# Tile by tile ahead of five norms: the last unit of a projection split in two, with VectorE squaring its own sums

## The chip, the cores and the metric

The kernel runs on one core of one Trainium2 chip. The metric is the device time of one execution in microseconds, given as the median of several runs. Every stage of the network runs in one launch, with the engines tied together by semaphores written by hand.

## What is computed

A stack of small transformer-like layers on a sequence of T = 256 tokens with D = 1024 channels, all in 32-bit floats. Between the stages the residual stream `x` goes through RMS norms:

```python
def _rmsnorm(x, g):
    xf = x.astype(jnp.float32)
    y = xf * lax.rsqrt(jnp.mean(xf * xf, axis=-1, keepdims=True) + EPS)
    return (y * g.astype(jnp.float32)).astype(x.dtype)
```

The parts around the change, with their norms as the kernel numbers them:

```python
x = x + gate_m * ((z @ w_glu_a) * sigmoid(z @ w_glu_b))              # glu, then norm 3
x = x + gate_f * (square(relu(h @ w_fc1)) @ w_fc2)                   # fc2_1, then norms 4 and 5 (norm_f, then the next block's)
h = h + mamba2_mixer(h, ...)                                         # ... @ out_w is ssm_out, then norm 6
h = h + sigmoid(rms_norm(h, ple_norm_w) @ gate_w) * (p @ proj_w)     # ple_gate_0, then norm 7
h = h + attention(h, ...)                                            # ... @ attn_out_w is attn_out, then norm 8
```

## The kernel before, in words

**Layout.** The residual stream `xT` is kept with channels on the 128 partitions: eight tiles `xT[:, k]` of 128x256. A projection's output is computed in units of two tiles (128 x 2 x 256, 512 values a partition, one PSUM bank). Weights arrive in blocks of 1024 x 256 in a ring of four. A matrix product in full precision is made of three products in a rounded format: ScalarE rounds a block (`round_to`, L869), VectorE takes the rest of it (`lower_to`, L2319, two instructions of 128x1024 a block), the same is done to the input, and TensorE runs high x high, high x low, low x high (`block_products`, L1473, L1494 to L1498). fc1_1 and fc2_1 do the first two as one product 512 wide (`wide_products`, L1506, L1520 and L1521), with each of a unit's two tiles in a bank of its own.

**Order inside a unit.** `project` (L1533) finishes the first tile before it starts the second. In ssm_out (L2165) and fc2_1 (L2051) the two tiles alternate at every k. The consumer of a unit waits for `blocks_done`, which rises when the last block of the unit is through, so it always sees both tiles at once.

**A norm.** When VectorE has added a unit to two tiles of `xT` (L2830 and L2834 in glu, L2390 in fc2_1, L3072 in `add_projection`, L3087 and L3089 in `embedding`), it raises `x_ready`. ScalarE then squares these two tiles (`square`, L918, one instruction of 128x512 at L926) and raises `sq_ready`. TensorE multiplies the squares by a matrix of ones (`norm_stats`, L1680, L1691), which sums over channels and leaves the sum on all partitions: eight tiles, each of two passes for an ordinary 32-bit product. For norms 0, 1, 2, 4, 6, 7 and 8 VectorE first adds the squares of the first units (`sum_squares`, L2397, with L2403 and L2406), so that TensorE has four tiles instead of eight; norm 3 has all eight. At norm 4 TensorE multiplies all eight tiles by other weights for the first of two norms (L1707) and uses the added squares for the second (L1711 to L1714). ScalarE takes Ln and Exp of the result (L943 or L941, L944) to make `rstd`, VectorE normalises the eight tiles (L2839, L2903, L2889, L2882), ScalarE rounds each (L889, L891), and TensorE's next block begins with the first rounded tile (`swept`, `swept_wide`).

**What stands in the queues around it.** The order on each engine is written out by hand. TensorE: at norms 6 and 8 it has products of the embedding (`ple_unit`, L2182) between the last block and the statistics. At norms 3, 4, 7 and 8 it has products that nobody reads (`idle_products`, L1675, L1678): four ahead of norm 7's statistics, five behind those of norms 3 and 7, two behind norm 4's, one behind norm 8's. ScalarE: at norm 3 it rounds the first block of fc1_1 and loads the table for Ln and Exp (L914) ahead of the four squares. At norm 7 it takes the Sigmoid of a unit (L1359) first, then loads the table, then squares. VectorE: the lowering of the next stage's first block stands ahead of the last unit in fc2_1 (`residual_halves`, L2378), and behind it at ssm_out and attn_out.

A few lines of the glu stage on VectorE, and of norm 3 on ScalarE:

```python
ps = unit("glu", 2 * n + 1)                                   # waits for the whole block
tt(glu_prod, ps, glu_gate, ALU.mult).then_inc(glu_mul, 1)     # L2830, 128x512
for i in range(2):                                            # L2834, two of 128x256
    ins = nc.vector.scalar_tensor_tensor(out=xT[:, k], in0=glu_prod[:, i], scalar=mod(1, GATE_M, k), in1=xT[:, k], ...)
ins.then_inc(x_ready, 1)

def norm_squares(i, version):
    log_and_exp()                                             # L914, a table load
    for p in range(4):
        square(i, version, p)                                 # L926, waits for x_ready
```

Of the kernel before, what the change touches and what calls it, by code (L numbers as in the profile page):

```python
# [10 lines left out]

# [221 lines left out]
def program(nc, dram, out):  # L233
# [8 lines left out]
    with ctx:  # L242
# [55 lines left out]
        STAT, MISC = PS[4], PS[5:8]  # L298
        SPARE = PS[3]
# [90 lines left out]
        hn_ready = sem("hn_ready")  # L390
        h_ready = sem("h_ready")
# [50 lines left out]
        rows_act = sem("rows_act")  # L442
        rows_dve = sem("rows_dve")
# [242 lines left out]

        def wide_units(phase, blocks_each, leaves):
# [25 lines left out]
        for layer, version in ((0, 7), (1, 9)):  # L713
# [14 lines left out]
            units(f"ple_gate_{layer}", 1, [(ple_sig, 4 * layer + n + 1) for n in range(4)])  # L728
# [129 lines left out]
        def _(act):  # L858
# [291 lines left out]
            ins.then_inc(rows_act, 1)  # L1150
# [83 lines left out]
            square(4, 4, 3)  # L1234
# [96 lines left out]
            def embedding(phase, layer, norm, version):  # L1331
                for p in range(4):
                    round_to(ready[first_unit[phase] + p] + 1 if p < 3 else first_block[f"ple_gate_{layer}"] + 1)
                    square(norm, version, p)
# [17 lines left out]
                for n in range(4):  # L1352
# [13 lines left out]
            square(7, 7, 3)  # L1366
# [92 lines left out]
        def _(pe):  # L1459
# [13 lines left out]
            def block_products(phase, n, arrived, places):  # L1473
# [29 lines left out]
                if places[-1][2].stop == NB:  # L1503
                    last.then_inc(blocks_done, 1)

            def wide_products(phase, n, arrived, places):  # L1506
# [4 lines left out]
                for k, ps, columns, x_high, x_low, start, stop in places:  # L1511
# [4 lines left out]
                    if arrived and columns.start == 0:  # L1516
# [5 lines left out]
                                            start=False, stop=stop, skip_group_check=True)  # L1522
                last.then_inc(blocks_done, 1)
# [9 lines left out]
            def project(phase, n, x, arrived=None, unit=None, order=range(KB)):  # L1533
# [4 lines left out]
                                for i in range(2) for k in order])  # L1538

# [140 lines left out]
            def norm_stats(i):  # L1680
# [17 lines left out]
            def two_norm_stats():  # L1698
# [5 lines left out]
                for k in range(DT):  # L1704
                    if k % 2 == 0:
# [242 lines left out]
            pe.wait_ge(rows_act, 1)  # L1948
            pe.wait_ge(rows_dve, 1)
# [99 lines left out]
            for n in range(4):  # L2049
                ps = wide_banks("fc2_1", n)  # L2050
                for kb in range(4):  # L2051
                    tile = split_arrived("fc2_1", 2) if n == 0 else None
                    wide_products("fc2_1", 4 * n + kb, (lambda k: tile(KB * kb + k)) if tile else None,
                                  [(k, ps[i], slice(P * i, P * i + P), hid_high[:, KB * kb + k], hid[:, KB * kb + k],
                                    kb == 0 and k == 0, kb == 3 and k == KB - 1)
                                   for k in range(KB) for i in range(2)])
# [103 lines left out]
            for kb in range(2):  # L2160
                for n in range(4):
                    if kb == 0:
                        banks.append(pair(start_unit("ssm_out", n)))
                    arrived = split_arrived("ssm_out") if n == 0 else None
                    block_products("ssm_out", 4 * kb + n, (lambda k: arrived(KB * kb + k)) if arrived else None,  # L2165
                                   [(k, banks[n][:, i], slice(P * i, P * i + P), at_tile((y_high, xs), KB * kb + k),
                                     kb == 0 and k == 0 and i == 0, kb == 1 and k == KB - 1)
                                    for k in range(KB) for i in range(2)])
# [17 lines left out]
            def embedding(layer, norm):  # L2186
# [1096 lines left out]
```

## Time and profile before

| | |
|---|---|
| median of 3 runs | 1170.21 us (1169.49 to 1174.09) |
| the profiled execution, its own time | 1172.47 us |
| its span, first to last instruction | 1170.6 us |
| mean granted TensorE clock | 0.982 |
| TensorE busy (matmul) | 1113.4 us, 95% of the span |
| VectorE busy | 829.1 us, 71% |
| ScalarE busy | 558.1 us, 48% |
| GpSimd busy | 45.0 us, 4% |
| DMA, mean | 210 GB/s |

The time of an execution is 1.87 us longer than the span of its profile. Matmuls are pipelined: an instruction's duration overlaps the next one's, so the distance between starts is what counts. A matmul of 32-bit operands shows as two passes (x2). In the chain of waits, each line has a start, the time that this piece adds to the chain, and what it was.

### The profile page before, as it was taken

To read this page: it belongs to the slowest core of one execution; us is meant where nothing else is said; L and a number is where in the kernel's file an instruction comes from. 1 tells how busy PE (TensorE), PEld (TensorE's weight loads), DVE (VectorE), ACT (ScalarE), POOL (GpSimd) and SP (SyncE) were. 2 spreads that over 40 slices of the span, in tenths; PEclk is the share of its full clock that TensorE was granted. 3 is DMA by queue.
4 is the path that set the end of the run, shared out by engine and by line. 5 is a ranking of instruction groups with operands and counts; after the bars stand their busy time and mean duration, and the time that the engine had idled before them with its cause. 6 is when DMAs were issued, how large, how long until landed. Compare 5 with 4: busy or idle time off the path is not lost.

```text
span 1170.6 us, 21137 instructions
## 1 busy us (share of the span) xinstructions
PE 1113.4 (95%) x8970; PEld 971.9 (83%) x8970; DVE 829.1 (71%) x1414; ACT 558.1 (48%) x876; POOL 45.0 (4%) x71
## 2 busy tenths in 40 slices
PE   7899898999999997879999999999989999999998
PEld 4788676988888885469988888899978899988898
DVE  1699466877578674875677764578898966659955
ACT  3224633445101124653555543456677846467944
POOL 0010011000000000000000000000000000042000
PEclk9999998999999998999999999989999999999999
DMA  9977688899848957865455555525432345343342
GB/s 374 377 279 270 229 327 305 306 333 329 342 181 251 346 191 157 329 246 180 144 180 184 187 194 190 180 80 173 158 130 78 133 151 180 130 152 117 107 145 72
DMA packets 38287, 246.41 MB, mean 210 GB/s; under 512 B 4400, under 2 KB 5584, under 8 KB 9648
## 3 DMA queue, kind: packets, MB, share of 16 engines
q1 hardware_dynamic: 29072, 182.36, 45.8%
q0 software_dynamic: 6240, 43.94, 9.9%
q10 hardware_dynamic: 2880, 18.74, 3.9%
q8 instruction: 71, 1.16, 0.4%
q14 instruction: 24, 0.20, 0.1%
HBM read 225.24 MB, written 19.79 MB: 209 GB/s over the span
## 4 chain that ended last, share of the span: by engine, by line
PE 78%; DVE 10%; DMA 5%; ACT 4%; issue 2%; SPq 0%; ACTq 0%; DVEq 0%
PE ps L1494 11%; PE ps L1498 10%; PE ps L1496 10%; PE ps L1520 10%; PE ps L1501 10%; PE ps L1521 5%; PE ps L1645 4%; DMA ca_dram<-more 2%; PE ps L1738 1%; DMA more<-in_ada_w 1%; PE ps L2182 1%; PE ps L1593 1%; DVE ada_more L2974 1%; PE ps L1691 1%; PE ps L1871 1%
## 5 line engine op out<-in xcount | busy, mean ns | idle before, releaser
L1494 PE MATMUL ps<-rounded_parts,w_high_rounded 128*128 128x256 f32 x1136 | 328.9, 290 | 2.2 <-DVE rounded_parts L2335 1.3
L2328 DVE TENSOR_TENSOR ring_rounded<-ring,w_high_rounded 128x1024 fp32r<-128x1024 f32 x220 | 260.8, 1227 | 88.9 <-ACT w_high_rounded L882 88.5
L1496 PE MATMUL ps<-rounded_parts,w_high_rounded 128*128 128x256 f32 x1136 | 322.9, 284 | 0.0
L1498 PE MATMUL ps<-rounded_parts,ring_rounded 128*128 128x256 f32 x1136 | 322.8, 284 | 0.0
L882 ACT ACTIVATE w_high_rounded<-ring 128x1024 fp32r<-128x1024 f32 x220 | 219.8, 1049 | 63.8 <-PE ps L1521 48.2
L1494 PEld LDWEIGHTS ps<-rounded_parts,w_high_rounded 128*128 128x128 f32 x1136 | 219.6, 193 | 11.4 <-issue 6.7
L1496 PEld LDWEIGHTS ps<-rounded_parts,w_high_rounded 128*128 128x128 f32 x1136 | 219.6, 193 | 0.2
L1498 PEld LDWEIGHTS ps<-rounded_parts,ring_rounded 128*128 128x128 f32 x1136 | 219.4, 193 | 0.0
L1520 PE MATMUL ps<-rounded_parts,w_high_rounded 128*128 128x512 f32 x496 | 175.3, 399 | 0.0
L1521 PE MATMUL ps<-rounded_parts,ring_rounded 128*128 128x256 f32 x496 | 139.3, 281 | 0.0
L1501 PE MATMUL ps<-big,ring 128*128 128x256 f32 x544 | 121.0, 381 | 0.0
L1501 PEld LDWEIGHTS ps<-big,ring 128*128 128x128 f32 x544 | 102.1, 190 | 14.7 <-issue 1.2
L1520 PEld LDWEIGHTS ps<-rounded_parts,w_high_rounded 128*128 128x128 f32 x496 | 93.2, 188 | 23.3
L1521 PEld LDWEIGHTS ps<-rounded_parts,ring_rounded 128*128 128x128 f32 x496 | 93.7, 189 | 0.0
L2460 DVE SCALAR_TENSOR_TENSOR big<-big,cols 128x256 f32<-128x256 f32 x120 | 48.0, 479 | 0.0
L1079 ACT ACTIVATE we_t<-ps 128x512 f32<-128x512 f32 x32 | 17.4, 596 | 58.0 <-PE ps L1871 58.0
L1501 PE MATMUL ps<-hT,ring 128*128 128x256 f32 x192 | 42.7, 381 | 0.0
L1501 PEld LDWEIGHTS ps<-hT,ring 128*128 128x128 f32 x192 | 36.1, 190 | 6.4 <-issue 1.2
L1060 ACT ACTIVATE big<-ps 128x512 f32<-128x512 f32 x16 | 9.6, 598 | 64.8 <-PE ps L1498 55.4
L2928 DVE SCALAR_TENSOR_TENSOR ada_w<-ada_w,cols 128x256 f32<-128x256 f32 x72 | 29.6, 482 | 8.4 <-ACT ada_w L1254 8.4
L1645 PE MATMUL ps<-ada_w,ada_more 128*32 128x256 f32 x432 | 29.3, 389 | 4.1 <-DMA ada_w<-in_ada_w 4.1
L926 ACT ACTIVATE sq<-xT 128x512 f32<-128x512 f32 x24 | 14.3, 623 | 36.4 <-DVE xT L3072 27.4
(426 smaller groups left out, 1555.1 us busy)
## 6 DMA issues: line engine op xcount, KB each, us to landing
ring<-in_blocks SPq DMA_DIRECT2D x139, 1024.0 KB, 4.9
ada_w<-in_ada_w POOLq DMA_DIRECT2D x27, 1024.0 KB, 7.5
ada_more<-in_ada_w POOLq DMA_DIRECT2D x13, 1024.0 KB, 7.5
we_dram<-we_t ACTq DMA_DIRECT2D x8, 1024.0 KB, 7.8
ca_dram<-more ACTq DMA_DIRECT2D x8, 1024.0 KB, 10.8
ring<-we_dram SPq DMA_DIRECT2D x8, 1024.0 KB, 5.7
ring<-ca_dram SPq DMA_DIRECT2D x8, 1024.0 KB, 7.2
big<-in_ada_w SPq DMA_DIRECT2D x4, 1024.0 KB, 11.3
```

The lines of the kernel that those rows point to most:

```text
L882: nc.scalar.activation(w_high[:, c % 2, ks], ring[:, b % RING, ks], ACT.Copy)\
L1079: nc.scalar.activation(we_t[:, 2 * b:2 * b + 2].rearrange("p g r x -> p (g r x)"), MISC[b % 2][:, :], ACT.Copy).then_inc(we_copied, 1)
L1494: nc.tensor.matmul(out, high[:, k, columns], x_high, start=start, stop=False, skip_group_check=True)
L1496: nc.tensor.matmul(out, high[:, k, columns], x_low, start=False, stop=False, skip_group_check=True)
L1498: last = nc.tensor.matmul(out, low[:, k, columns], x_high, start=False, stop=stop, skip_group_check=True)
L1501: last = nc.tensor.matmul(out, w[:, k, columns], x, start=start, stop=stop, skip_group_check=True)
L1520: nc.tensor.matmul(ps[:, :], w_hi[:, k, columns], both, start=start, stop=False, skip_group_check=True)
L1521: last = nc.tensor.matmul(ps[:, T * first:T * first + T], w_lo[:, k, columns], rounded(x_high), start=False, stop=stop, skip_group_check=True)
L1645: last = nc.tensor.matmul(bank[j:j + COPIES, 0:NB], c_spread[:, k, PIECES - 1 - piece:PIECES - 1 - piece + COPIES], w[:, k], start=(piece ...
L2328: nc.vector.tensor_tensor(rounded(w), w, w_high[:, c % 2, ks], ALU.subtract)\
L2460: ins = nc.vector.scalar_tensor_tensor(out=conv[:, k], in0=apad[:, k, tap:tap + T], scalar=w, in1=conv[:, k], op0=ALU.mult, op1=ALU.add)
L2928: ins = nc.vector.scalar_tensor_tensor(out=dst, in0=src[:, i, tap:tap + T], scalar=w, in1=dst, op0=ALU.mult, op1=ALU.add)
```

## The change

The last unit ahead of norms 3, 4, 6, 7 and 8 is computed and consumed tile by tile.

TensorE finishes the first tile of the unit's last block before the second, and raises a new semaphore, `tile_done`. Except in fc2_1, where it has been so, the second tile goes into another bank (`LAST_TILE`, the first half of bank 7). VectorE waits for the first tile alone, adds it to `xT` and squares it itself (`square_tile`), and does the same with the second when the block is done. ScalarE's square of the last two tiles goes. At ple_gate_0 ScalarE's Sigmoid of the last unit is two of 128x256. TensorE's statistics wait for each of the two last squares. Norm 3 joins the norms whose first six squares are added up by VectorE; that sum stands ahead of the tile work. In fc2_1 the lowering of the first xbc block moves behind the last unit. Two semaphores of the S5 stage become one.

```diff
+        LAST_TILE = MISC[2][:, 0:T]
...
-        sq_before = (0, 4, 8, 12, 16, None, 20, 24, 28)
-        summed = {0: 3, 1: 3, 2: 2, 4: 3, 6: 3, 7: 3, 8: 3}
-        sums_until = {i: n + 1 for n, i in enumerate(summed)}
+        sq_before = (0, 4, 8, 12, 15, None, 18, 21, 24)
+        summed = {0: 3, 1: 3, 2: 2, 3: 3, 4: 3, 6: 3, 7: 3, 8: 3}
+        TAILS = (3, 4, 6, 7, 8)
+        tail_of = {i: n + 1 for n, i in enumerate(TAILS)}
+        sums_until = {i: n + 1 + 2 * sum(t < i for t in TAILS) for n, i in enumerate(summed)}
...
             def norm_squares(i, version):
                 log_and_exp()
-                for p in range(4):
+                for p in range(3 if i in TAILS else 4):
                     square(i, version, p)
...
             log_and_exp()
-            square(4, 4, 3)
             norm_rstd(4)
...
-                    square(norm, version, p)
+                    if p < 3:
+                        square(norm, version, p)
...
-                    ps = unit(f"ple_gate_{layer}", n)
                     if n >= 2:
                         act.wait_ge(ple_mul, 4 * layer + n - 1)
+                    if layer == 0 and n == 3:
+                        act.wait_ge(tile_done, tail_of[7])
+                        nc.scalar.activation(ple_gate[:, 1, 0:T], bank_of(first_unit["ple_gate_0"] + 3)[:, 0:T],
+                                             ACT.Sigmoid).then_inc(ple_sig, 1)
+                        unit("ple_gate_0", 3)
+                        nc.scalar.activation(ple_gate[:, 1, T:2 * T], LAST_TILE, ACT.Sigmoid).then_inc(ple_sig, 1)
+                        continue
+                    ps = unit(f"ple_gate_{layer}", n)
...
             log_and_exp()
-            square(7, 7, 3)
             norm_rstd(7)
...
+                    if tail and stop and columns.start == 0:
+                        last.then_inc(tile_done, 1)
                 last.then_inc(blocks_done, 1)
...
+            def project_tail(phase, n, x):
+
+                outs = start_unit(phase, n)[:, 0:T], LAST_TILE
+                tile_products(phase, n, [[(k, outs[i], slice(P * i, P * i + P), at_tile(x, k), k == 0, k == KB - 1)
+                                          for k in range(KB)] for i in range(2)])
+
+            def tile_products(phase, n, halves):
+
+                block_products(phase, n, None, halves[0]).then_inc(tile_done, 1)
+                block_products(phase, n, None, halves[1])
...
                     if k == 0 and i in summed:
                         pe.wait_ge(sq_sum, sums_until[i])
+                    elif i in TAILS and k >= 6:
+                        pe.wait_ge(sq_sum, sums_until[i] + k - 5)
                     elif k % 2 == 0:
...
-            for n in range(8):
+            for n in range(7):
                 project("glu", n, (sq, mixT), split_arrived("glu", 2) if n == 0 else None)
+            project_tail("glu", 7, (sq, mixT))
             norm_stats(3)
...
-                                   for k in range(KB) for i in range(2)])
+                                   for k, i in sorted(itertools.product(range(KB), range(2)),
+                                                      key=lambda at: at[1] if tail else 0)], tail)
...
+                    outs = [banks[n][:, 0], LAST_TILE if n == 3 else banks[n][:, 1]]
...
+                    if kb == 1 and n == 3:
+                        tile_products("ssm_out", 4 * kb + n, halves)
...
+                    elif layer == 0 and n == 3:
+                        project_tail("ple_gate_0", 3, (sq, hT))
...
+            project_tail("attn_out", 3, (att_high, mixT))
...
+            def square_tile(i, k):
+
+                nc.vector.tensor_tensor(squares(i)[:, k], xT[:, k], xT[:, k], ALU.mult).then_inc(sq_sum, 1)
+
+            def tail_tile(i, phase, n, first):
+
+                if first:
+                    dve.wait_ge(tile_done, tail_of[i])
+                    return bank_of(first_unit[phase] + n)[:, 0:T]
+                dve.wait_ge(blocks_done, ready[first_unit[phase] + n])
+                return LAST_TILE
...
                 dve.wait_ge(glu_sig, n + 1)
+                if n == 3:
+                    sum_squares(3)
+                    dve.wait_ge(x_ready, 8 + 3)
+                    for i in range(2):
+                        ins = tt(glu_prod[:, i], tail_tile(3, "glu", 7, i == 0), glu_gate[:, i], ALU.mult)
+                        if i:
+                            ins.then_inc(glu_mul, 1)
+                            dve.wait_ge(glu_mul, 4)
+                        else:
+                            link(ins)
+                        ins = nc.vector.scalar_tensor_tensor(out=xT[:, 6 + i], in0=glu_prod[:, i],
+                                                             scalar=mod(1, GATE_M, 6 + i), in1=xT[:, 6 + i],
+                                                             op0=ALU.mult, op1=ALU.add)
+                        if i:
+                            ins.then_inc(x_ready, 1)
+                            dve.wait_ge(x_ready, 8 + 4)
+                        else:
+                            link(ins)
+                        square_tile(3, 6 + i)
+                    continue
...
             sum_squares(4, final_sum)
-            residual_halves("fc2_1", gate_f1, 3, 4)
+            lower_to(ready[first_unit["fc2_1"] + 6])
+            for i in range(2):
+                if i == 0:
+                    dve.wait_ge(tile_done, tail_of[4])
+                else:
+                    dve.wait_ge(blocks_done, ready[first_unit["fc2_1"] + 6])
+                for half in range(2):
+                    ins = nc.vector.scalar_tensor_tensor(out=xT[:, 6 + i], in0=bank_pair("fc2_1", 3)[:, i, half],
+                                                         scalar=gate_f1(6 + i), in1=xT[:, 6 + i], op0=ALU.mult, op1=ALU.add)
...
+                square_tile(4, 6 + i)
...
-                for n in range(4):
+                for n in range(3):
                     nc.vector.tensor_tensor(xT[:, 2 * n:2 * n + 2], xT[:, 2 * n:2 * n + 2], unit(phase, n), ALU.add)\
                         .then_inc(x_ready, 1)
-                    if n == 2:
-                        sum_squares(norm)
+                sum_squares(norm)
+                for i in range(2):
+                    ins = nc.vector.tensor_tensor(xT[:, 6 + i], xT[:, 6 + i], tail_tile(norm, phase, 3, i == 0), ALU.add)
...
+                    square_tile(norm, 6 + i)
```

In `embedding` on VectorE the last unit of layer 0 becomes the same per tile: product with the gate (128x256), sum into `xT`, `square_tile(7, 6 + i)`, each waiting for the one before. `wait_ge(rows_act, 1)` and `wait_ge(rows_dve, 1)` become `wait_ge(rows_copied, 2)`.

## Rows read from the trace of the kernel before

**Rows 1.** The page: busy time and instructions; the chain's shares by engine.

```profile
PE 1113.4 (95%) x8970; PEld 971.9 (83%) x8970; DVE 829.1 (71%) x1414; ACT 558.1 (48%) x876; POOL 45.0 (4%) x71
...
PE 78%; DVE 10%; DMA 5%; ACT 4%; issue 2%; SPq 0%; ACTq 0%; DVEq 0%
```

**Rows 2.** The chain in order of time at norms 3, 4, 6, 7, 8: start, us, what.

```profile
567.53 3.49 PE ps L1691 x16
...
755.48 3.55 PE ps L1707 x16
...
976.63 3.46 PE ps L2182 x16
980.09 1.73 PE ps L1691 x8
...
1012.23 2.16 PE ps L1678 x10
...
1136.46 1.73 PE ps L1691 x8
```

**Rows 3.** Timeline of ScalarE at norm 3: start us, us, instruction [idle before <-releaser].

```profile
564.32 1.28 ACT L914 ACT_TABLE_LOAD   x1
565.61 1.68 ACT L926 ACTIVATE big<-xT 128x512 f32<-128x512 f32 x3
569.21 0.63 ACT L926 ACTIVATE big<-xT 128x512 f32<-128x512 f32 x1 [1.93 <-DVE xT L2834]
```

**Rows 4.** Timeline of VectorE ahead of norms 3, 4 and 6.

```profile
563.45 2.36 DVE L2328 TENSOR_TENSOR ring_rounded<-ring,w_high_rounded 128x1024 fp32r<-128x1024 f32 x2 [3.52 <-ACT w_high_rounded L882]
...
751.02 2.36 DVE L2328 TENSOR_TENSOR ring_rounded<-ring,w_high_rounded 128x1024 fp32r<-128x1024 f32 x2 [3.29 <-ACT w_high_rounded L882]
...
972.29 0.69 DVE L2403 TENSOR_TENSOR sq<-sq 128x512 f32<-128x512 f32 x1 [0.70 <-ACT sq L926]
973.02 0.69 DVE L2406 TENSOR_TENSOR sq<-sq 128x512 f32<-128x512 f32 x1
```

**Rows 5.** Groups by line and form on VectorE: xcount | busy us, mean ns | idle.

```profile
L2961 DVE TENSOR_TENSOR more<-ps,we_t 128x256 f32<-128x256 f32 x16 | 5.9, 420 | 0.4 <-PE ps L2067 0.4
...
L2834 DVE SCALAR_TENSOR_TENSOR xT<-more,mods,xT 128x256 f32<-128x256 f32 x8 | 3.5, 482 | 0.1
```

**Rows 6.** Timeline of TensorE and ScalarE at norm 7.

```profile
1008.14 1.89 PE L1678 MATMUL ps<-const 128*128 128x256 f32 x8
1009.87 1.03 PE L1691 MATMUL ps<-big,const 128*128 128x256 f32 x4
1011.10 1.13 PE L1691 MATMUL ps<-big,const 128*128 128x256 f32 x4 [0.21 <-ACT big L926]
...
1010.42 0.63 ACT L926 ACTIVATE big<-xT 128x512 f32<-128x512 f32 x1 [0.18 <-DVE xT L3089]
```

**Rows 7.** Timeline of ScalarE at norms 4, 6 and 8: the last squares.

```profile
757.21 0.63 ACT L926 ACTIVATE sq<-xT 128x512 f32<-128x512 f32 x1 [3.67 <-DVE xT L2390]
...
977.39 0.63 ACT L926 ACTIVATE sq<-xT 128x512 f32<-128x512 f32 x1 [3.23 <-DVE xT L3072]
...
1135.49 0.63 ACT L926 ACTIVATE sq<-xT 128x512 f32<-128x512 f32 x1 [3.23 <-DVE xT L3072]
```

**Rows 8.** Stretches: us, PE, PEld, DVE, ACT, POOL busy (x), granted clock, DMA share, GB/s.

```profile
560.00:567.50 7.50, 7.50 (x64) 7.50 (x64) 2.36 (x2) 5.45 (x7) 0.00 (x0) 1.00 0.42 146
...
874.00:876.00 2.00, 0.74 (x4) 0.54 (x6) 2.00 (x4) 2.00 (x3) 0.00 (x0) 0.80 0.70 274
876.00:878.00 2.00, 2.00 (x12) 1.10 (x10) 2.00 (x3) 1.97 (x3) 0.00 (x0) 0.50 0.53 221
...
882.00:884.00 2.00, 2.00 (x18) 2.00 (x18) 2.00 (x4) 2.00 (x3) 0.00 (x0) 0.99 0.00 0
```

**Rows 9.** Timeline of TensorE: first products after two gaps elsewhere.

```profile
505.97 0.77 PE L2002 MATMUL ps<-const,big 128*128 128x128 f32 x5 [1.88 <-ACT big L1182]
...
875.26 1.13 PE L2090 MATMUL ps<-ada_more,more 128*64 128x256 f32 x4 [2.30 <-DVE ada_more L3021]
```

More of the change, by code:

```diff
@@ L12 @@
+import itertools
 from contextlib import ExitStack
@@ L390, in program @@
         hn_ready = sem("hn_ready")
+        tile_done = sem("tile_done")
         h_ready = sem("h_ready")
@@ L685, in units, with gates_until @@
                 left.append(leave)
+        def gates_until(layer, n):
+            return 5 * layer + n + 1 + (layer == 0 and n == 3)
         def wide_units(phase, blocks_each, leaves):
@@ L727, in program @@
                 ready[first_unit[f"ple_proj_{layer}"] + i] = first_block[f"ple_proj_{layer}"] + 1
-            units(f"ple_gate_{layer}", 1, [(ple_sig, 4 * layer + n + 1) for n in range(4)])
+            units(f"ple_gate_{layer}", 1, [(ple_sig, gates_until(layer, n)) for n in range(4)])
         units("final", 0, [(out_copied, n + 1) for n in range(4)])
@@ L1504, in block_products, with wide_products @@
                     last.then_inc(blocks_done, 1)
-            def wide_products(phase, n, arrived, places):
+                return last
+            def wide_products(phase, n, arrived, places, tail=False):
                 b = first_block[phase] + n
@@ L2052, in _ @@
                     tile = split_arrived("fc2_1", 2) if n == 0 else None
+                    tail = n == 3 and kb == 3
                     wide_products("fc2_1", 4 * n + kb, (lambda k: tile(KB * kb + k)) if tile else None,
@@ L2164, in _ @@
                     arrived = split_arrived("ssm_out") if n == 0 else None
[L2165 to L2168, printed above, removed]
+                    outs = [banks[n][:, 0], LAST_TILE if n == 3 else banks[n][:, 1]]
+                    halves = [[(k, outs[i], slice(P * i, P * i + P), at_tile((y_high, xs), KB * kb + k),
+                                kb == 0 and k == 0 and (i == 0 or n == 3), kb == 1 and k == KB - 1) for k in range(KB)]
+                              for i in range(2)]
+                    if kb == 1 and n == 3:
+                        tile_products("ssm_out", 4 * kb + n, halves)
+                    else:
+                        block_products("ssm_out", 4 * kb + n, (lambda k: arrived(KB * kb + k)) if arrived else None,
+                                       [place for both in zip(*halves) for place in both])
                     if kb == 0 and n < 2:
@@ L3070, in add_projection @@
                 dve.wait_ge(x_ready, 4 * (norm - 1))
-                for n in range(4):
+                for n in range(3):
                     nc.vector.tensor_tensor(xT[:, 2 * n:2 * n + 2], xT[:, 2 * n:2 * n + 2], unit(phase, n), ALU.add)\
                         .then_inc(x_ready, 1)
-                    if n == 2:
-                        sum_squares(norm)
+                sum_squares(norm)
+                for i in range(2):
+                    ins = nc.vector.tensor_tensor(xT[:, 6 + i], xT[:, 6 + i], tail_tile(norm, phase, 3, i == 0), ALU.add)
+                    if i:
+                        ins.then_inc(x_ready, 1)
+                        dve.wait_ge(x_ready, 4 * norm)
+                    else:
+                        link(ins)
+                    square_tile(norm, 6 + i)
             add_projection("ssm_out", 6)
@@ L3083, in embedding @@
                     lower_to(first_block[f"ple_gate_{layer}"] + min(n + 2, 4))
-                    dve.wait_ge(ple_sig, 4 * layer + n + 1)
+                    if layer == 0 and n == 3:
+                        for i in range(2):
+                            dve.wait_ge(ple_sig, 4 + i)
+                            a = ple_prod[:, 6 + i]
+                            ins = nc.vector.tensor_tensor(a, a, ple_gate[:, 1, T * i:T * i + T], ALU.mult)
+                            if i:
+                                ins.then_inc(ple_mul, 1)
+                                dve.wait_ge(ple_mul, 4)
+                            else:
+                                link(ins)
+                            ins = nc.vector.tensor_tensor(xT[:, 6 + i], xT[:, 6 + i], a, ALU.add)
+                            if i:
+                                ins.then_inc(x_ready, 1)
+                                dve.wait_ge(x_ready, 28)
+                            else:
+                                link(ins)
+                            square_tile(7, 6 + i)
+                        continue
+                    dve.wait_ge(ple_sig, gates_until(layer, n))
                     g = ple_gate[:, n % 2].rearrange("p (k n) -> p k n", k=2)
```

20 lines of the change are left out of this document (13 added, 7 removed).

## The prediction, made before the change was run

> **What bounds the kernel now.** I read the page first, then the chain of waits in order of time, then the timelines of each engine around the five norms, and last the granted clock. On the page TensorE is busy 95% of the span and holds 78% of the chain that ended last, VectorE only 10% and ScalarE 4% [rows 1]. So an edit on VectorE or ScalarE is worth only what it takes out of TensorE's waits, and these stand in the stretches between a projection's last block and the next one. In the chain these stretches are TensorE's too [rows 2]. At norms 6 and 8 TensorE works off products of the embedding (3.46 us at norm 6) and then four tiles of statistics, 1.73 us for 8 passes, so one tile costs 0.43 us. At norm 3 it works off all eight tiles (16 passes) in 3.49 us, at norm 4 in 3.55 us; eight tiles without a wait are 2 x 1.73 = 3.46 us. Only norm 7 shows a wait: its first two tiles end at 1010.90, the last two start at 1011.10 and take to 1012.23 [rows 6].
>
> **Norm 7** (the embedding's gate unit 3). Now: block ends about 1008.30, then four idle products and two tiles (1008.14 to 1010.90), and ScalarE's squares end at 1010.42 + 0.63 = 1011.05 [rows 6]; the last two tiles end 1.18 us later. After: the first tile's Sigmoid, product, sum and square lie under the block's second half. For the second tile ScalarE's half-width Sigmoid is some 0.4 us (estimate: 0.42 us is what VectorE needs for this width [rows 5]; ScalarE needs 0.63 for a whole one [rows 6]), then VectorE has a product, a sum and a square of 128x256, each 0.42 us with 0.04 us to the next dependent one [rows 4, 5]: squares stand at 1008.30 + 0.4 + 3 x 0.46 = 1010.1. TensorE starts its tiles only at 1008.30 + 1.73 (four idle products at 0.43) = 1010.03 and reaches the last one 1.3 us after that, so nothing is waited for: end 1010.03 + 1.73 = 1011.76 against 1012.23. **Gain 0.47 us.** What ends last next is the five idle products behind (2.16 us [rows 2]) and the K/V projection after them; both move with it.
>
> **Norm 4** (fc2_1). Now TensorE's eight tiles take 3.55 instead of 3.46 us: ScalarE's squares end at 757.21 + 0.63 = 757.84, just when TensorE wants them [rows 2, 7]. After, they are ready earlier, but TensorE still has its eight tiles: **gain 0.09 us**, and no more. The change also moves the lowering of xbc block 0, 2.36 us, from 751.02 [rows 4], where VectorE was idle, to behind the tail. The tail's second tile is two dependent scalings (0.52 each) and a square (0.46) from 755.5: 757.0; dt_w's lowering 0.4, then 2.36: about 759.8. The normalising waits for rstd, which comes some 1.0 us after the statistics' end at 755.48 + 3.55 = 759.03, thus 760.0. It is hidden with 0.2 us to spare; without cover it costs what it overruns. The swapped order of products inside block 15 costs nothing: same count, and its operands were lowered before the block began.
>
> **Norms 6 and 8.** Squares end at 977.39 + 0.63 = 978.02 and at 1135.49 + 0.63 = 1136.12 [rows 7]. TensorE takes up the first tile of statistics at 980.09 and 1136.46 and the fourth 1.3 us later [rows 2]. They were hidden by 1.7 us and more; making them 0.5 us earlier is worth **0**. The same holds for the second tile's own bank and for the joined semaphore (two waits for one).
>
> **Norm 3** (glu unit 7) is where the sum is decided. The change adds norm 3 to those whose first six tiles VectorE adds up to two, and it puts this sum ahead of the tile work in VectorE's queue. The sum needs ScalarE's three squares; these stand behind a table load at 564.32 (1.28 us) and run 565.61 to 567.29 [rows 3]. The block itself ends at 567.53, its first tile, 24 of its 48 products earlier (64 in 7.5 us, 0.12 us each [rows 8]), at 567.53 - 2.8 = 564.7. So VectorE, free from 565.81 [rows 4], sits behind that wait until 567.3: the first tile is not done meanwhile. Then, strictly in order: two linked sums of 128x512, each 0.69, 0.73 apart [rows 4]: to 568.75. First tile, from 568.67 (its product is independent of the sum, and such an instruction starts 0.08 before the end of the one ahead: in scaling's row four pairs of 2 x 0.48 cover 3.5 us, 0.88 a pair [rows 5]): product 0.46, scaling 0.48 + 0.04 = 0.52, square 0.34: 1.32, to 570.0. Second tile: product 0.46, scaling 0.52, square 0.42: 1.40, to 571.4. From the squares to the end of the statistics norm 7's row gives 1.18 us for two tiles, 0.43 less for one: 0.75. End 572.15. Before it was 567.53 + 3.49 = 571.02. **Loss 1.1 us.** TensorE has 4 x 0.43 = 1.7 us less to do here, but all of that becomes idle time. Behind it every step (Ln, Exp, eight normalisings, roundings, the swept block) moves by the same; the five idle products move too. Bounds: 0.8 us if the three independent instruction starts each overlap by 0.08, 1.5 us if each of the eight steps costs 0.05 more.
>
> The Trainium skill (Perfetto Trace Analysis, Optimizing Scalar/DVE Operations) puts VectorE's per-instruction overhead at some 60 ns from SBUF and 125 ns from PSUM, and advises larger operations. By the rows halving costs more: 2 x 0.42 against 0.69 us [rows 4, 5] is 0.15 us per split operation. With the page's figures the three splits of norm 3 would cost 0.25 us, not 0.46, and the loss there would be 0.9 us; the measured rows decide.
>
> **Sum.** 1.1 - 0.47 - 0.09 = +0.5 us. The profiled execution took 1172.47 us, of which the span is 1170.6; the sum would make it 1173.0. It lies 2.3 us above the median of three, 1170.21, so on the scale of the runs the forecast is **1170.7 us**. The three runs lie 4.6 us apart; a measurement of this kernel can tell some 0.5% (5.9 us) from no change, so this is "no change".
>
> **Rivals.**
> *Every hand-off counts* (faster). The hop to ScalarE and half of each wide operation leave the path at all five norms. From block end to squares: norm 3 2.31 to 1.44, norm 4 2.36 to 1.49, norm 6 and 8 1.39 to 0.93, norm 7 2.75 to 1.8: together 3.6 us, 1166.6 us. For it: those intervals are real [rows 3, 4, 6, 7]. Against it: TensorE is not idle in them [rows 2], and at norm 3 the order in VectorE's queue. Chance 0.1.
> *Norm 3 comes out even* because VectorE is at the first tile in time, and norms 7 and 4 gain: -0.5 us, 1169.7 us. It decides if the squares come before 566. ScalarE's rows speak against it [rows 3]. Chance 0.1.
> *The clock falls at norm 3* (slower). In this trace TensorE went from the granted clock 1.00 (2.4 GHz) to 0.50 (1.2 GHz) at about 875.2, after 2.30 us idle, and stayed there until about 882 [rows 8, 9]; 1.88 us idle at 504 to 505.97 brought none [rows 9]. Norm 3 had practically no idle time before; after the change it has 1.2 us before the first tile, 0.5 before the third and 0.8 before the fourth, 2.5 us in all with 1.3 us of products between. Had it fallen, the last tile and five idle products would take double: 0.43 + 2.16 = 2.6 us more, 1173.3 us. It decides if the pieces of idle time count as one gap. Chance 0.2; that a low spell goes on into the next blocks (up to half of 6.8 us = 3.4) is in the range. The Trainium skill (TensorE: Matmul & The Clock Gate, HAM oscillation) says that the gate follows how busy TensorE has just been and that idle gaps between bursts bring it down; it bears on this rival, and the trace agrees.
> *It doesn't do what it says*: at norm 3, that is the forecast itself (the first tile isn't done meanwhile); at the other four it does, hidden or nearly so.
>
> **How the numbers follow.** Forecast 0.6, the rivals 0.1, 0.1 and 0.2. The range is 1167.0 to 1174.3: below it lies most of the first rival, above it a clock fall with a long spell; it also takes in the spread of the runs. Faster by over 0.5% (under 1164.4) needs more than all hand-offs together: 0.02. Slower by over 0.5% (over 1176.1) needs the clock fall to last into the next stage and a disturbed run as well: 0.04. Within: 0.94.
>
> **What would show it.** In the profile after: at norm 3 VectorE's two sums of squares start about 567.3 (after ScalarE's third square, not after a block), TensorE's last statistics product ends about 1.1 us later against the end of the block than 3.49, with 8 passes instead of 16 and idle time between them. At norm 7 the eight passes run without a gap and end 0.5 us sooner. At norms 4, 6 and 8 the chain's pieces on TensorE keep their lengths within 0.1 us. I am wrong if norm 3's stretch is shorter than before, if one of norms 4, 6 and 8 shortens by over 0.3 us, or if the granted clock in the stretch behind norm 3 is below 1.00.

## The result, and the profile after

The changed kernel takes 1177.77 us (median of 7 runs, 1174.73 to 1181.40) against 1170.21 us (7 runs, 1167.28 to 1176.76): ratio 1.006, 95% interval 1.0041 to 1.0079. It is slower, by 5 to 9 us; the forecast was 1170.7 us, with 1174.3 us as the upper end of its range. The profiled execution took 1179.18 us, its span is 1177.3 us (before: 1170.6).

Whole times of this kernel scatter by several us. The end of the last glu block, which comes before anything that matters here, lies anywhere between 563.93 and 570.52 us in the nine profiles of this study, with the same code ahead of it but for one wait in the S5 stage and, in two variants, three squares in ScalarE's idle time. So each stage is measured from a point of its own. For norm 3 that is the **stretch** from the end of the last glu product to the first product of fc1_1's second block. It is 580.06 - 567.53 = 12.53 us before and 587.64 - 568.95 = 18.69 us after. In the variant that leaves norm 3 alone it comes out within 0.01 us of before.

| from ... to | before | after | difference |
|---|---|---|---|
| start to the last glu block's end | 567.53 | 568.95 | +1.42 |
| norm 3: block's end to the statistics' end | 3.50 | 4.66 | +1.16 |
| statistics' end to the low products of fc1_1's first block | 5.21 | 8.61 | +3.40 |
| these to fc1_1's second block | 3.82 | 5.42 | +1.60 |
| norm 4: eight tiles of statistics | 3.55 | 3.45 | -0.10 |
| norm 7: block's end to the statistics' end | 3.93 | 3.46 | -0.47 |
| norms 6 and 8: statistics | 1.73 | 1.73 | 0 |

The chain in order of time, changed kernel, at norms 4, 6, 7 and 8 (start, us, what):

```profile
763.05 3.45 PE ps L1739 x16
...
987.17 1.73 PE ps L1721 x8
...
1015.38 1.73 PE ps L1706 x8
1017.11 1.73 PE ps L1721 x8
1018.84 2.16 PE ps L1706 x10
...
1143.07 1.73 PE ps L1721 x8
```

Compare with [rows 2]. From norm 4 on, the starts lie 7.57, 7.08, 6.61 (norm 7's idle products, at 1012.23 before) and 6.61 us behind those of before. So the loss is all there by norm 4, norm 7 gives back 0.47 us, and norms 6 and 8 change nothing. Of 7.57 us, 1.42 had been there at the last glu block; 6.15 us come from norm 3's stretch. The step from 7.57 to 7.08 is norm 4's 0.10 us and a difference in low clock in the xbc stage (the projection behind norms 4 and 5): 48 small products there take 5.67 us before and 5.28 us after.

VectorE's timeline in the changed kernel, from norm 3 on:

```profile
568.81 0.69 DVE L2445 TENSOR_TENSOR big<-big 128x512 f32<-128x512 f32 x1 [7.46 <-ACT big L934]
569.54 0.69 DVE L2448 TENSOR_TENSOR big<-big 128x512 f32<-128x512 f32 x1
570.15 0.42 DVE L2885 TENSOR_TENSOR more<-ps,more 128x256 f32<-128x256 f32 x1
...
571.12 0.42 DVE L2453 TENSOR_TENSOR big<-xT 128x256 f32<-128x256 f32 x1
...
572.43 0.42 DVE L2453 TENSOR_TENSOR big<-xT 128x256 f32<-128x256 f32 x1
574.60 3.26 DVE L2913 SCALAR_TENSOR_TENSOR hT<-xT,gains,rstd 128x256 f32<-128x256 f32 x8 [1.75 <-ACT rstd L952]
...
580.94 4.63 DVE L2370 TENSOR_TENSOR ring_rounded<-ring,w_high_rounded 128x1024 fp32r<-128x1024 f32 x4
```

The first row is as forecast: the sums wait for ScalarE's squares. What is new is the wait's length, 7.46 us. Before, VectorE used that time for two lowerings of 128x1024, the row at 563.45 in [rows 4]. Here they are missing, and stand in the last row, at 580.94, behind the eight normalisings and the eight low parts (the row's other two are the second block's).

TensorE's timeline in the same stretch:

```profile
570.37 1.92 PE L1721 MATMUL ps<-big,const 128*128 128x256 f32 x6 [1.42 <-DVE big L2448]
572.91 0.70 PE L1721 MATMUL ps<-big,const 128*128 128x256 f32 x2 [0.61 <-DVE big L2453]
...
575.77 3.21 PE L1646 MATMUL ps<-rounded_parts,w_high_rounded 128*128 128x256 f32 x16
582.22 3.21 PE L1652 MATMUL ps<-rounded_parts,ring_rounded 128*128 128x256 f32 x16 [3.23 <-DVE ring_rounded L2370]
585.22 2.58 PE L1657 MATMUL ps<-rounded_parts,w_high_rounded 128*128 128x256 f32 x16
```

The same three passes in the kernel before:

```profile
573.19 3.21 PE L1618 MATMUL ps<-rounded_parts,w_high_rounded 128*128 128x256 f32 x16
576.24 2.07 PE L1624 MATMUL ps<-rounded_parts,ring_rounded 128*128 128x256 f32 x16
578.14 2.08 PE L1629 MATMUL ps<-rounded_parts,w_high_rounded 128*128 128x256 f32 x16
```

The swept block goes over the block's high part first (L1646), then its low part (L1652): 16 products each, eight for each of two tiles (the expectations below say "eight products" for such a pass). The low part is what the lowering makes, and TensorE stands 3.23 us for it. L1652 and L1657 then take 3.21 and 2.58 us, where the kernel before had 2.07 and 2.08. The stretches show why (the third column from the right is the granted clock):

```profile
580.00:582.00 2.00, 0.00 (x0) 0.00 (x0) 2.00 (x4) 0.32 (x1) 0.00 (x0) 1.00 0.00 0
582.00:584.00 2.00, 1.78 (x11) 1.79 (x12) 2.00 (x3) 0.00 (x0) 0.00 (x0) 0.74 0.00 0
584.00:586.00 2.00, 2.00 (x11) 2.00 (x11) 1.57 (x2) 0.00 (x0) 0.00 (x0) 0.50 0.00 0
586.00:588.00 2.00, 2.00 (x17) 1.96 (x16) 0.00 (x0) 0.16 (x1) 0.00 (x0) 0.90 0.00 0
```

TensorE is idle through 580 to 582, and from 583 it runs at 1.2 GHz, until about 586.4.

In the kernel before, the lowering of fc1_1's first block was no line of its own. It happened inside `unit("glu", 7)`, which calls `lower_to(ready[u] + 1)` ahead of its wait, and that end reaches one block beyond the unit, into the next stage. `tail_tile`, which replaces `unit` there, only waits. In fc2_1 `residual_halves`, which reached one block further in the same way, was written out with a shorter reach, and xbc's first block is lowered later too; there the diff shows it.

### The profile page after: what moved, and what is told of

Same layout as the page of the kernel before. It is cut to its first block, busy times and chain, and to the rows that moved or that the text cites. A ratio compares the mean times of both kernels' runs of the same rounds, so it can differ in the third digit from the quotient of the medians.

```text
span 1177.3 us, 21133 instructions
## 1 busy us (share of the span) xinstructions
PE 1112.3 (94%) x8962; PEld 970.4 (82%) x8962; DVE 835.4 (71%) x1431; ACT 555.1 (47%) x872; POOL 45.0 (4%) x71
## 3 DMA queue, kind: packets, MB, share of 16 engines
q8 instruction: 71, 1.16, 0.4%
## 4 chain that ended last, share of the span: by engine, by line
PE 74%; DVE 12%; DMA 6%; ACT 5%; issue 2%; SPq 0%; ACTq 0%; DVEq 0%
PE ps L1508 10%; PE ps L1535 10%; PE ps L1512 10%; PE ps L1510 10%; PE ps L1515 10%; PE ps L1536 5%; PE ps L1673 3%; DMA ca_dram<-more 2%; DVE ring_rounded L2370 1%; PE ps L2221 1%; DMA w_high<-in_blocks 1%; PE ps L1621 1%; DVE ada_more L3062 1%; DMA more<-in_ada_w 1%; PE ps L1903 1%
## 5 line engine op out<-in xcount | busy, mean ns | idle before, releaser
L1226 ACT ACTIVATE ada_more<-ps 128x512 f32<-128x512 f32 x16 | 9.6, 598 | 47.6 <-PE ps L1536 40.1
```

## The experiments

**Theory A**: the lowering came late; TensorE waits 3.23 us for it, and the clock falls because of that wait. **Theory B**: the clock falls because TensorE idles between norm 3's statistics, my rival with the clock. **Theory C**: the second tile's bank or the order of the tiles costs on TensorE.

### lower_first: the lowering back in its place

```diff
                 if n == 3:
+                    lower_to(first_block["fc1_1"] + 1)
                     sum_squares(3)
```

> The changed kernel with one line more: VectorE lowers the first block of fc1_1 ahead of the sum of squares of norm 3, where the kernel before did it. Theory A (the lowering came late: 3.23 us of wait ahead of L1652, and the clock fell because of that wait): the wait before the low products of fc1_1's first block is gone, the granted clock stays at 1.00 there, and the time from the last glu product's end to fc1_1's second block is 12.5 us of the kernel before plus 1.1 to 1.2 us, 13.7 us, against 18.7 us in the changed kernel. Whole time about 5 us under the changed kernel, 0.5 us over the one before: ratio to before 0.998 to 1.003. Theory B (the clock falls because TensorE idles between the statistics of norm 3): the clock still falls, and at least 1.7 us of the loss stay: 15.4 us or more for the stretch. Theory C (the second tile's bank or the tile order slow TensorE down): the loss stays whole.

Measured: 1171.15 us (12 runs) against 1170.60 us of the kernel before (32 runs), ratio 1.0011, interval 0.9995 to 1.0026. The stretch is 581.36 - 567.71 = 13.65 us. VectorE and TensorE in this kernel:

```profile
563.63 2.36 DVE L2370 TENSOR_TENSOR ring_rounded<-ring,w_high_rounded 128x1024 fp32r<-128x1024 f32 x2 [3.53 <-ACT w_high_rounded L890]
567.50 0.69 DVE L2445 TENSOR_TENSOR big<-big 128x512 f32<-128x512 f32 x1 [1.51 <-ACT big L934]
```

```profile
571.60 0.70 PE L1721 MATMUL ps<-big,const 128*128 128x256 f32 x2 [0.61 <-DVE big L2453]
...
574.47 3.22 PE L1646 MATMUL ps<-rounded_parts,w_high_rounded 128*128 128x256 f32 x16
577.52 2.08 PE L1652 MATMUL ps<-rounded_parts,ring_rounded 128*128 128x256 f32 x16
```

The lowering is under the wait again, L1652 follows L1646 without a gap and takes 2.08 us, and the granted clock is 1.00 from 560 to 590. TensorE still idles between the statistics (1.36 us, some 0.5 and 0.61 us) and the clock stays, so theory B falls. The second tile's bank and the order of the tiles are still the changed ones, so theory C falls with it. One line takes 5.04 of the 6.16 us away. What stays is 1.12 us.

### before_late_lowering: this alone, in the kernel before

```diff
-                ps = unit("glu", 2 * n + 1)
+                if n == 3:
+                    dve.wait_ge(blocks_done, ready[first_unit["glu"] + 7])
+                    ps = pair(bank_of(first_unit["glu"] + 7))
+                else:
+                    ps = unit("glu", 2 * n + 1)
```

> The kernel before with nothing of the change but the lowering of fc1_1's first block moved behind norm 3's normalising, as the changed kernel has it. Theory A: TensorE waits about 3.2 us between the first and the second eight products of fc1_1's first block, and if the clock falls in that wait 1.7 us more go at 1.2 GHz: the stretch from the last glu product's end to fc1_1's second block grows from 12.5 to 15.7 (clock stays) or 17.4 us (clock falls). Whole time 3 to 5 us over the kernel before: ratio 1.002 to 1.005. Theories B and C: the stretch stays at 12.5 us and the ratio at 1.000.

Measured: 1175.61 us (7 runs), ratio 1.0044, interval 1.0026 to 1.0061. The stretch is 584.42 - 565.99 = 18.43 us, 1.0 us over the longer of the two forecasts. TensorE and the granted clock:

```profile
578.15 3.78 PE L1624 MATMUL ps<-rounded_parts,ring_rounded 128*128 128x256 f32 x16 [3.23 <-DVE ring_rounded L2328]
```

```profile
576.00:578.00 2.00, 0.00 (x0) 0.00 (x0) 2.00 (x4) 0.26 (x1) 0.00 (x0) 0.67 0.00 0
578.00:580.00 2.00, 1.85 (x8) 1.85 (x9) 2.00 (x3) 0.00 (x0) 0.00 (x0) 0.50 0.00 0
580.00:582.00 2.00, 2.00 (x12) 2.00 (x11) 1.50 (x2) 0.00 (x0) 0.00 (x0) 0.50 0.00 0
582.00:584.00 2.00, 2.00 (x13) 2.00 (x13) 0.00 (x0) 0.00 (x0) 0.00 (x0) 0.62 0.00 0
```

The same 3.23 us of wait, with nothing of the tile work in the kernel. The clock fell inside the wait here and stayed down until about 583.5, so from the low products to the second block it cost 6.27 - 3.82 = 2.45 us, where it cost 1.60 us in the changed kernel. The late lowering alone costs 18.43 - 12.53 = 5.90 us in the stretch, against 6.16 us of the whole change, with a longer spell of low clock. By the whole times it is slower as well.

### norm3_as_before: the other four norms alone

The glu unit, `summed`, `TAILS` and VectorE's branch for `n == 3` go back to what they were:

```diff
-        summed = {0: 3, 1: 3, 2: 2, 3: 3, 4: 3, 6: 3, 7: 3, 8: 3}
-        TAILS = (3, 4, 6, 7, 8)
+        summed = {0: 3, 1: 3, 2: 2, 4: 3, 6: 3, 7: 3, 8: 3}
+        TAILS = (4, 6, 7, 8)
...
-            for n in range(7):
+            for n in range(8):
                 project("glu", n, (sq, mixT), split_arrived("glu", 2) if n == 0 else None)
-            project_tail("glu", 7, (sq, mixT))
```

> The changed kernel with the glu unit and norm 3 as in the kernel before; norms 4, 6, 7 and 8 stay tile by tile. Theory A and my sum: the stretch at norm 3 is that of before (12.5 us), norm 4's eight tiles take 3.46 us instead of 3.55, norm 7's statistics end 0.47 us sooner, norms 6 and 8 keep their lengths: 0.56 us under the kernel before in the stretches, ratio 0.997 to 1.001. A rival in which splitting the last unit costs at every norm (more instructions, the other bank): 0.3 us or more over before at each of norms 4, 6 and 8.

Measured: 1170.60 us (10 runs), ratio 0.9997, interval 0.9981 to 1.0014. The stretch is 12.54 us, norm 4's statistics take 3.45 us, norm 7's four tiles follow its idle products without a gap (3.46 us for both), norms 6 and 8 have 1.73 us each. Splitting the unit costs nothing at these four, and brings 0.57 us.

### wait_filled: products that nobody reads in the wait

```diff
                     for i in range(2):
                         nc.tensor.matmul(ps[i][:, T:2 * T], high[:, k, P * i:P * i + P], x_high[:, k], start=(k == 0),
                                          stop=False, skip_group_check=True)
+                idle_products(3, 7)
                 for k in range(KB):
```

> The changed kernel with seven products that nobody reads (0.43 us each, 3.0 us) between the first and the second eight products of fc1_1's first block, where TensorE waits 3.23 us for the late lowering. If idle time in that wait brings the clock down: the granted clock stays at 1.00, the wait itself stays (VectorE is not faster), and the stretch from the last glu product's end to fc1_1's second block falls from 18.69 by 1.77 us to 16.9 us. If the clock falls for another reason (the gaps between norm 3's statistics): it still falls and the stretch is 18.7 us or, since the fillers run at 1.2 GHz too, more.

Measured: 1174.96 us (10 runs), ratio 1.0035, interval 1.0014 to 1.0056. TensorE and the granted clock where the wait had been:

```profile
575.76 3.18 PE L1707 MATMUL ps<-const 128*128 128x256 f32 x14
579.16 1.10 PE L1653 MATMUL ps<-rounded_parts,ring_rounded 128*128 128x256 f32 x7 [0.21 <-DVE ring_rounded L2371]
```

```profile
576.00:578.00 2.00, 2.00 (x11) 1.77 (x10) 2.00 (x6) 1.26 (x2) 0.00 (x0) 1.00 0.03 8
578.00:580.00 2.00, 1.79 (x12) 1.34 (x11) 2.00 (x2) 0.00 (x0) 0.00 (x0) 1.00 0.00 0
```

The low products start 13.27 us after the block's end, as in the changed kernel, and the clock stays at 1.00. The stretch is 17.37 us, 1.32 less than the changed kernel's and 0.5 us over the 16.9 that I expected. I had given the clock 1.77 us, and the changed kernel's remainder was only 1.60 us longer than an undisturbed one. The other 0.28 us against the 3.82 us of an undisturbed remainder is a second small wait: VectorE's lowering of the block's other half comes 1.2 us after the first, and TensorE at 2.4 GHz uses up its eight products in under 1 us. So of the 1.60 us, 0.28 us are again the late lowering's, and 1.32 of the 6.16 us are the clock's. Nothing but the filling differs from the changed kernel, so this speaks for the idle wait as what brought the clock down. It rests on one profile of each kernel, and whether a shorter wait brings the clock down differs from execution to execution (last section).

### tile_then_sum: the first tile under the wait for the squares

This is lower_first with the sum of squares moved between the two tiles; TensorE's first statistics wait for one more count.

```diff
-                    sum_squares(3)
                     dve.wait_ge(x_ready, 8 + 3)
                     for i in range(2):
+                        if i:
+                            sum_squares(3)
...
-                        pe.wait_ge(sq_sum, sums_until[i])
+                        pe.wait_ge(sq_sum, sums_until[i] + (i == 3))
```

> lower_first with VectorE's work at norm 3 in another order: product, scaling and square of the first tile, then the two sums of the six squares, then the second tile. VectorE is free some 1.5 us before ScalarE's three squares are there, so the first tile's 1.3 us go under that wait: statistics end 1.3 us sooner than in lower_first, at 3.3 us after the block's end instead of 4.59, and the stretch is 12.35 us instead of 13.65. If the wait for the squares did not hide it (first tile not done in time), the stretch stays at 13.65.

Measured (one run, 1165.92 us, which says little by itself): the stretch is 12.37 us, the statistics end 3.33 us after the block. VectorE:

```profile
562.14 0.42 DVE L2887 TENSOR_TENSOR more<-ps,more 128x256 f32<-128x256 f32 x1
...
563.11 0.42 DVE L2453 TENSOR_TENSOR big<-xT 128x256 f32<-128x256 f32 x1
563.72 0.69 DVE L2445 TENSOR_TENSOR big<-big 128x512 f32<-128x512 f32 x1 [0.19 <-ACT big L934]
```

The first tile ends at 563.53, before the block's end at 563.93: it is done "meanwhile", as the change has it. The order in VectorE's queue was worth 1.28 us, and with it norm 3 is 0.16 us better than before, in this one profile.

### early_squares: the squares where ScalarE waits anyway

lower_first's line, and ScalarE squares the first six tiles ahead of the Sigmoid of glu unit 6, VectorE sums them ahead of its wait for that Sigmoid.

```diff
             for n in range(4):
+                if n == 3:
+                    round_to(ready[first_unit["glu"] + 6] + 1)
+                    for p in range(3):
+                        square(3, 3, p)
                 ps = unit("glu", 2 * n)
...
-            norm_stats(3, 3)
+            log_and_exp()
+            norm_rstd(3)
...
-                dve.wait_ge(glu_sig, n + 1)
                 if n == 3:
                     sum_squares(3)
+                dve.wait_ge(glu_sig, n + 1)
+                if n == 3:
+                    lower_to(first_block["fc1_1"] + 1)
```

> The changed kernel with the lowering in its old place, and norm 3's first three squares taken by ScalarE where it waits for glu unit 6 (from 558.1 in the trace of before, when the third unit has been added), so that VectorE sums them before the last unit and can work on its first tile while TensorE computes the second. Theory A: the last tile's product, scaling and square end 1.44 us after the block, the statistics 0.75 us later, 2.2 us after the block's end against 3.5 before and 4.66 in the changed kernel: the stretch is 12.5 - 1.3 = 11.2 us. With norms 4 and 7 that is 1.9 us under the kernel before: ratio 0.996 to 1.000. If ScalarE's work, not the statistics, sets the swept block's start, or the products that nobody reads do, the stretch stays near 12.5 us.

Measured: 1169.09 us (12 runs), ratio 0.9986, interval 0.9969 to 1.0004. The stretch is 11.25 us, and the statistics end 2.20 us after the block's end at 566.53:

```profile
566.37 1.46 PE L1726 MATMUL ps<-big,const 128*128 128x256 f32 x6
568.03 0.70 PE L1726 MATMUL ps<-big,const 128*128 128x256 f32 x2 [0.20 <-DVE big L2458]
```

TensorE works through the sums and the first tile's squares at once and waits 0.20 us for the last square. That is 1.28 us better than before in the stretch and 7.44 us better than the changed kernel. fewer_idle, which has the same code here, gives 11.25 us again. By the whole times early_squares isn't told from the kernel before.

### fewer_idle: two and three products instead of four and five at norm 7

```diff
-                idle_products(i, {7: 4}.get(i, 0))
+                idle_products(i, {7: 2}.get(i, 0))
...
-                    idle_products(i, 5)
+                    idle_products(i, 3 if i == 7 else 5)
```

> early_squares with fewer products that nobody reads at norm 7: two instead of four ahead of the statistics, three instead of five behind them. The last square of norm 7 stands 1.07 us before TensorE takes it up in the changed kernel, so two products less ahead (0.86 us) are all gained; behind, the first normalised tile is there 1.45 us after the statistics' end and five products take 2.16, so two less gain 0.7 us. From the gate block's end to the K/V projection's first product 5.61 us become 4.1. Ratio to before 0.996 to 0.998, 1.5 us under early_squares. If the clock needs these products it falls behind norm 7, and 1.7 us or more are lost instead.

Measured: 1169.35 us (12 runs) against 1171.22 us (23 runs), ratio 0.9984, interval 0.9966 to 1.0003. TensorE from the gate block's end at 1003.81:

```profile
1004.51 1.89 PE L1726 MATMUL ps<-big,const 128*128 128x256 f32 x8
1006.24 1.46 PE L1711 MATMUL ps<-const 128*128 128x256 f32 x6
1008.03 7.14 PE L1520 MATMUL ps<-mixT,ring 128*128 128x256 f32 x32 [0.33 <-DVE mixT L2977]
```

The K/V projection starts 4.22 us after the gate block's end, against 5.61 us in early_squares; the granted clock is 1.00 from 1003 to 1020. The 1.39 us are real in the stretch and lie under the scatter of the whole times, whose ratio is that of early_squares and not below it, as I had expected. By the stretches both versions beat both kernels: at norm 3 they are 1.28 us shorter than the kernel before, at norm 7 (from the gate block's end to the K/V projection, 6.09 us before) 0.48 and 1.87 us, and at norms 4, 6 and 8 not longer.

## Why the prediction was wrong, and where it was right

**The step that failed** is a sentence in the part on norm 3: "So VectorE, free from 565.81 [rows 4], sits behind that wait until 567.3". The row gives VectorE as busy to 565.81 with two lowerings of 128x1024. I took it for work that stays. It was fc1_1's first block, and it stood there only because `unit("glu", 7)` lowers up to `ready[u] + 1`. The change takes that call out. My own list of what stands in VectorE's queue names fc2_1, ssm_out and attn_out and leaves glu out. I had gone through the same question at norm 4, where the diff writes out a new `lower_to` and so shows that something was moved, and had costed it. At norm 3 the diff writes nothing, and I didn't ask what `unit` did besides waiting. No rival covered it. The forecast was +0.5 us; the working had nothing for the 3.23 us of wait nor for the clock behind it. lower_first, which puts the call back, takes 5.04 us of the loss away. A time over 1176.1 us had been given a chance of 0.04, and for another reason.

**The terms that were in the sum** came out close:
- Norm 3's statistics: +1.1 us forecast (end 4.62 us after the block), +1.16 measured in the changed kernel (4.66), +1.09 in lower_first (4.59). The sums waited for ScalarE's squares, and tile_then_sum and early_squares show that the order and the late squares cost this, not the splitting.
- Norm 7: -0.47 forecast, -0.47 measured. Norm 4: -0.09 forecast, -0.10 measured. Norms 6 and 8: 0 and 0.
- Their sum, +0.5 us, is what lower_first has in its stretches: 1.12 - 0.47 - 0.10 = +0.55 us, ratio 1.0011 with an interval that holds it.
- The moved lowering at norm 4: forecast to end 0.2 us before `rstd`. VectorE's timeline in the changed kernel:

```profile
764.82 2.35 DVE L2370 TENSOR_TENSOR ring_rounded<-ring,w_high_rounded 128x1024 fp32r<-128x1024 f32 x2
767.50 3.26 DVE L2991 SCALAR_TENSOR_TENSOR hT<-xT,s_small,rstd 128x256 f32<-128x256 f32 x8 [0.33 <-ACT rstd L952]
```

It ended 0.33 us before. The same move that was free here cost 5.04 us at norm 3 by lower_first, and 5.90 us by before_late_lowering. At norm 4 it came before the normalising; at norm 3 the next `lower_to` in VectorE's queue is behind the normalising and the eight low parts.

**The rival with the clock** had a mechanism that exists and the wrong place. TensorE's idle time between norm 3's statistics (1.42, 0.61 and some 0.5 us between them) left the granted clock at 1.00, in the changed kernel, lower_first and wait_filled. The clock fell in or just behind the 3.23 us wait that follows, and did so in both kernels that had this wait unfilled; with the wait filled it did not fall. Its price, 1.32 us by wait_filled, was less than the 2.6 us of the rival. So one of the signs of being wrong came, the granted clock below 1.00 behind norm 3, but from a wait that the prediction did not have. Its reading that 1.88 us of idle time brings no fall is one execution's: in fewer_idle the clock fell at 506.9 us, 1.5 us after the same wait (1.89 us).

**The sum against the runs.** The stretches add up to 6.16 - 0.47 - 0.10 = +5.6 us, ratio 1.0048, inside the interval of 1.0041 to 1.0079. The profile's own difference, 6.7 us, also holds +1.42 us from ahead of the last glu block, and later spells of low clock that differ from one execution to the next (in the xbc stage 6.8 us before, 3.4 us after). That the first of these comes from the change is not shown: other kernels with the same code there reach the last glu block at 563.93 to 570.52. norm3_as_before has the changed code of the S5 stage too and comes out at a ratio of 0.9997 (0.9981 to 1.0014), so a loss there is at most some 2 us (1.6 us by the interval's upper end, and the 0.57 us that norms 4 and 7 give back). It stays open whether some tenths of the median come from there.

## What to carry to other kernels

Where a change replaces a helper's call, list everything that the helper issues, not what its name says. A helper that waits and first issues work for the next stage is a place in a queue; with it gone, the work falls to the next call, however far behind. For each instruction that stood ahead of a wait before, look for its place in the new order, also where the diff shows no line of it. When an engine is given work early "meanwhile", read what stands ahead of it in its queue: at norm 3 the sum's wait for late squares turned the overlap into a loss, and moving these squares into ScalarE's idle time turned it into a gain in the stretch (1.28 us, too little to tell in the whole times).

## What the runs showed of the hardware

- A wait of 3.23 us on TensorE brought the granted clock from 1.00 to 0.50 in both kernels that had it, one profile each. In one it fell inside the wait, in the other 0.8 us after its end, and the remainder of the block took 2.45 and 1.60 us longer. The Trainium skill (TensorE: Matmul & The Clock Gate, HAM oscillation) says that waits between bursts of products bring the clock down; the trace agrees for this wait. In the one profile with products that nobody reads in the wait, the clock stayed at 1.00 (wait_filled).
- 1.42 us of idle time and two shorter pieces behind it did not bring it down, in two profiles (changed kernel, wait_filled), nor did 1.36 us and the same two pieces in lower_first.
- Between these, the same wait did it in some executions only. Eight of the nine profiles have a wait of 2.63 to 2.66 us in the last part of the S5 stage, ahead of glu. The clock fell within 0.3 us of its end in four of them and stayed at 1.00 in the other four. The kernel before, then the changed kernel, each with the stretch behind the wait:

```profile
513.42 0.66 PE L2033 MATMUL ps<-big,hT 128*32 128x128 f32 x8 [2.64 <-ACT ada_more L1174]
515.00:516.00 1.00, 1.00 (x25) 0.97 (x21) 1.00 (x1) 1.00 (x2) 0.00 (x0) 0.50 0.75 303
...
515.79 0.64 PE L2064 MATMUL ps<-big,hT 128*32 128x128 f32 x8 [2.65 <-ACT ada_more L1182]
516.00:517.00 1.00, 1.00 (x32) 0.85 (x28) 0.00 (x0) 0.78 (x2) 0.00 (x0) 1.00 0.91 352
```

- Idle time is not the only thing ahead of a fall. In all nine profiles the clock falls during the 48 products of 128x32 in the xbc stage, or just behind them, for 3.4 to 10.2 us. In the kernel before TensorE is busy from 768 to 774 without a gap, and the clock falls at 772.8:

```profile
770.00:772.00 2.00, 2.00 (x20) 2.00 (x20) 0.00 (x0) 0.00 (x0) 0.00 (x0) 1.00 1.01 426
772.00:774.00 2.00, 2.00 (x15) 2.00 (x15) 0.18 (x1) 0.00 (x0) 0.00 (x0) 0.70 0.10 37
```

- With all but the same code ahead of it, the end of one block lay within 6.6 us over nine profiles, while a stretch of 12.5 us behind it repeated within 0.01 us where its code was the same, and so did one of 11.25 us.
